# Order within an attention phase: transposes directly behind the scores, then corrections and outputs, then dense work

## The chip, the cores and the metric

The kernel runs on one core of one Trainium2 chip. Its time is the device time of one execution in microseconds. The kernel before took 1176.37 us in the median of 3 runs (1174.56 to 1176.48).

## What is computed

One decoder layer on a sequence of 1024 tokens of width 1024, all in float32. Two token mixers share one input projection and are merged by gates:

```python
h = rmsnorm(x, ln_pre);  z = h @ w_in        # columns of both mixers and of all gates
ya = conformer_conv(c_val, c_glu, ...)       # depthwise convolution, 31 taps, LayerNorm, swish, projection
ya = (ya * silu(c_gate)) @ w_br_conv
yb = sliding_window_sink_attention(q, k, v, sinks, positions)
yb = (yb * silu(a_gate)) @ w_br_attn
m = sigmoid(g_conv) * ya + sigmoid(g_attn) * yb
x = x + rmsnorm(m @ w_out, ln_post)
x = x + sigmoid(x @ w_ple_gate) * (p @ w_ple_proj)
```

The attention has 16 query heads of 64, two key and value heads, a window of 128 and one sink per head. The sequence is cut into 8 blocks of 128 queries; a block sees its own 128 keys and the 128 before, masked to the window, so that each query sees just 128 keys.

## The kernel before, in words

Activations lie transposed: features on the 128 partitions, tokens along the free axis. Every dense product is made in three passes: the weights and the activations are each split into a rounded high part and a low rest, and high by high, low by high and high by low are summed. A tile of 128 output features is 8 weight blocks by 3 passes by 2 halves of 512 tokens, that is 48 matmuls (L457). 114 tiles follow one another, with weights loaded one tile ahead into two slots; ScalarE makes the high part (L818) and VectorE the low part (L1158).

The attention is woven into the dense work of one gate, c_gate: 8 dense tiles are cut into 16 halves of 24 matmuls (L727), and each half makes a *phase* with one attention step, `attention(p)` for p = 0 to 15. Phase p belongs to query block n = p // 2 and to the half g = p % 2 of the heads. One block of attention work passes through several phases:

- Phase p, TensorE: `scores(p, 0)` and `scores(p, 1)` (L645) write the scores into PSUM. Where VectorE or ScalarE still read the old scores, they wait.
- VectorE: maxima of the scores (L1376, L1379), with the sinks (L1385 to L1389). ScalarE: the exponentials (L962, L967). VectorE: `normalise(p)` divides by the sums, in two halves (L1403); each half adds one to `probs_ready`.
- Phase p+1, TensorE: `turn(p)` transposes the normalised probabilities in 16 instructions (L663). It waits for both halves of `normalise(p)` and, by `half_evicted(p)`, until ScalarE has copied the gate half of phase p out of PSUM (L991).
- ScalarE: `copy_turned(p)` copies the transposes to SBUF (L948, L950), and VectorE masks a part of them (L1414) for the corrections.
- Phase p+2, TensorE: `outputs(p)` makes the outputs: from block n = 1 on first 8 correction matmuls (L697, with the differences `vstep` of neighbouring values, which VectorE makes once, in L1440 to L1444), then 8 output matmuls (L702). It waits by `half_evicted(p + 1)`, for the copies and the masks of step p, and for the outputs of step p-1 to have been copied away. ScalarE copies the outputs out in `copy_outputs(p)` (L975), which waits for `outputs(p)` and for `turn(p + 1)`, because both write the same banks.

So in phase p TensorE has five kinds of work: scores of p, corrections and outputs of p-2, transposes of p-1, and the dense half (for which `half_evicted(p - 2)` must hold). Their order in the queue is written out by hand in `attention`. In phases 1 and 2 the transposes stand within the dense half (in front of its weight block 6 or 5) instead, and phase 2 makes `outputs(0)` directly behind its scores.

The engines run on their own queues and wait by semaphores. ScalarE's order in phase p is: gate half p-1 (L988, L991), in every second phase the next weights' high part, `copy_outputs(p - 2)`, `copy_turned(p - 1)`, `exps(p)`. VectorE's is: maxima of p, gate half p-1 (L1428), extras of single phases (rotary parts in 0 to 2, `vstep` in 3, `sums_lo` in 14), masks of p-1 with the low part of weights between, `normalise(p)`.

Of the kernel before, what the change touches and what calls it, by code (L numbers as in the profile page):

```python
# [71 lines left out]
def build(nc, dram):  # L72
    with ExitStack() as ctx:
# [188 lines left out]
        def gate_bank(p):  # L262

            return psg_banks[:, 3 * (p % 2), :]
# [9 lines left out]
        def turn_place(p, side, jp):  # L274

            if p == LAST_P:
                return 2 + side, jp * QUARTER
            if side == 0:
                return whole_bank(p), jp * QUARTER
            return bank_pair(p).start + jp, 0  # L280
# [165 lines left out]
        def _(pe):  # L446
# [203 lines left out]
            def turn(p):  # L650

                g = p % 2
                pe.wait_ge(probs_ready, 2 * p + 2)
                if p < LAST_P:
                    half_evicted(p)
                if p in (1, LAST_P):
                    pe.wait_ge(o_ready, p)
                for jp in range(2):
                    for h in range(4):
                        for side in range(2):  # L660
                            queries = slice(side * HD, side * HD + HD)
                            bank, first = turn_place(p, side, jp)
                            mm = nc.tensor.transpose(psg_banks[:, bank, first + h * HD:first + h * HD + HD],  # L663
                                                     probs[g][queries, 4 * jp + h, :], ident[queries, queries])
                mm.then_inc(turned, 1)

            def half_evicted(p):

                n, h = divmod(p, 2)
                if h == 0:  # L670
                    pe.wait_ge(half_free, n + 1)
                else:
                    pe.wait_ge(ps_free[n % 2], (C0 + n) // 2 + 5)

            def out_of(p, side, par):

                return psg_banks[par * HD:(par + 1) * HD, bank_pair(p + 1).start + side, QUARTER:HALF]

            def heads_of(turned_rows, par):

                return turned_rows.rearrange("p (jp par j) q -> p par jp (j q)", jp=2, par=2)[:, par]

            def outputs(p):

                n, g = divmod(p, 2)
                gs = slice(g * HD, (g + 1) * HD)
                if p < LAST_P:
                    half_evicted(p + 1)
                if p > 0:
                    pe.wait_ge(o_ready, p)  # L690
                if n > 0:
                    pe.wait_ge(pt_masked, 2 * p - 2)
                    pe.wait_ge(vstep_ready, 3)
                    for side in range(2):
                        rows = slice(side * HD, side * HD + HD)
                        for par in range(2):
                            nc.tensor.matmul(out_of(p, side, par), vstep[rows, n - 1, gs], heads_of(pt_prev[rows], par),  # L697
                                             start=True, stop=False)
                pe.wait_ge(pt_copied, 2 * p + 2)
                for side in range(2):  # L700
                    for par in range(2):
                        mm = nc.tensor.matmul(out_of(p, side, par), vmix[:, n, gs], heads_of(pt_all[:, side], par),  # L702
                                              start=(n == 0), stop=True)
                mm.then_inc(pv_done, 1)

            def attention(p):

                n, h = divmod(p, 2)
                t = C0 + n
                half = slice(h * HALF, (h + 1) * HALF)  # L710
                scores(p, 0)
                scores(p, 1)
                if p > 1:
                    outputs(p - 2)
                if p > 2:
                    turn(p - 1)
                if h == 0:
                    pe.wait_ge(w_lo_ready, t + PLE_STEPS + 1)
                if n == 0:
                    pe.wait_ge(ps_free[h], C0 // 2 + 4)  # L720
                else:
                    half_evicted(p - 2)
                for k in range(KT):
                    if (p, k) in ((1, 6), (2, 5)):
                        turn(p - 1)
                    for m, (w, r) in enumerate(((w_hi, h_hi), (w_lo, h_hi), (w_hi, h_lo))):
                        mm = nc.tensor.matmul(gate_bank(p), w[:, t % 2, k * P:(k + 1) * P], r[:, k, half],  # L727
                                              start=(k == 0 and m == 0), stop=(k == KT - 1 and m == 2))
                mm.then_inc((half_done, tile_done)[h], 1)

            for p in range(2 * NB):
                attention(p)
# [941 lines left out]
```

## Time and profile before

| | us |
|---|---|
| Time, median of 3 runs | 1176.37 |
| Profiled execution, its time | 1176.3 |
| Its span, first to last instruction | 1174.5 |
| TensorE matmuls busy | 1164.0 |
| VectorE busy | 837.9 |
| ScalarE busy | 377.3 |
| L727 in the chain that ended last | 7% of the span |
| Granted clock of TensorE, mean | 0.998 |

The profile shows one execution. Busy time is the time in which an engine has an instruction in work; matmuls overlap, so a busy TensorE can still lose time between them, and the distance from start to start tells more than a duration. The phases p = 0 to 15 run from 488.9 us to 636 us of the span.

### The profile page before, as it was taken

How to read it: one execution, taken by the hardware profiler on the slowest of the kernel's cores; microseconds unless marked ns; L12 is line 12 of the kernel's file. 1: busy time of each engine (PE TensorE's matmuls, PEld its weight loads, DVE VectorE, ACT ScalarE, POOL GpSimd, SP SyncE). 2: the span in 40 equal slices, each digit the busy share in tenths (PEclk: the TensorE clock that was granted, in tenths of full speed). 3: DMA queues.
4: the chain of work that ended last, by engine and by line, in shares of the span. 5: the costliest groups of instructions: out<-in, count | busy, mean ns of one | idle time of the engine just before them, and what ended most of it. 6: DMA issues, size and time to landing. Idle time of an engine off the chain costs nothing.

```text
span 1174.5 us, 16083 instructions
## 1 busy us (share of the span) xinstructions
PE 1164.0 (99%) x6304; PEld 947.3 (81%) x6304; DVE 837.9 (71%) x934; ACT 377.3 (32%) x670; POOL 17.4 (1%) x17
## 2 busy tenths in 40 slices
PE   9999999999999999989999999999999999999998
PEld 7788888888888888867777888888888888888886
DVE  6999999999999983788777674783233344357665
ACT  6431221221121122266665442341122112444331
POOL 1020000000000000000000000000000000000000
PEclk9999999999999999999999999999999999999999
DMA  9622122222222323212122111333232232434655
GB/s 353 267 90 71 55 88 72 62 81 71 71 72 77 93 54 87 53 55 73 38 73 74 36 54 36 107 107 90 89 107 89 90 107 88 127 115 139 210 164 179
DMA packets 35530, 116.40 MB, mean 99 GB/s; under 512 B 4480, under 2 KB 4992, under 8 KB 35488
## 3 DMA queue, kind: packets, MB, share of 16 engines
q1 hardware_dynamic: 25120, 82.29, 22.1%
q10 hardware_dynamic: 10368, 33.56, 8.6%
q8 instruction: 26, 0.43, 0.2%
q14 instruction: 16, 0.13, 0.0%
HBM read 92.10 MB, written 20.97 MB: 96 GB/s over the span
## 4 chain that ended last, share of the span: by engine, by line
PE 94%; DMA 2%; ACT 1%; DVE 1%; SPq 1%; issue 0%; POOL 0%; ACTq 0%; DVEq 0%
PE psg L457 81%; PE psg L727 7%; PE psg L702 1%; PE psb L645 1%; DMA k_raw<-positions 1%; DMA x_rows<-x_rows 1%; PE psg L663 1%; PE psg L697 1%; PE psg L506 1%; ACT probs L962 0%; DVE w_lo L1158 0%; SPq L366 0%; PE psb L530 0%; PE psb L540 0%; SPq L363 0%
## 5 line engine op out<-in xcount | busy, mean ns | idle before, releaser
L457 PE MATMUL psg<-h_hi,w_hi 128*128 128x512 f32 x768 | 237.1, 390 | 0.5 <-DVE w_lo L1158 0.5
L457 PE MATMUL psg<-h_hi,w_lo 128*128 128x512 f32 x768 | 236.6, 389 | 0.0
L457 PE MATMUL psg<-h_lo,w_hi 128*128 128x512 f32 x768 | 236.4, 389 | 0.0
L818 ACT ACTIVATE w_hi<-w_raw 128x1024 fp32r<-128x1024 f32 x112 | 118.5, 1058 | 223.7 <-PE psg L457 211.4
L1158 DVE TENSOR_TENSOR w_lo<-w_raw,w_hi 128x1024 fp32r<-128x1024 f32 x114 | 139.1, 1221 | 70.0 <-ACT w_hi L818 69.9
L457 PEld LDWEIGHTS psg<-h_hi,w_hi 128*128 128x128 f32 x768 | 143.7, 188 | 31.1 <-issue 1.6
L457 PEld LDWEIGHTS psg<-h_hi,w_lo 128*128 128x128 f32 x768 | 144.2, 188 | 30.1
L457 PEld LDWEIGHTS psg<-h_lo,w_hi 128*128 128x128 f32 x768 | 144.1, 188 | 30.1
L1298 DVE SCALAR_TENSOR_TENSOR conv<-u,cols,conv 128x1024 f32<-128x1024 f32 x120 | 154.0, 1284 | 0.0
L1298 DVE SCALAR_TENSOR_TENSOR work<-u,cols,work 128x1024 f32<-128x1024 f32 x112 | 145.5, 1299 | 0.0
L727 PE MATMUL psg<-h_hi,w_hi 128*128 128x512 f32 x128 | 52.1, 407 | 0.0
L727 PE MATMUL psg<-h_hi,w_lo 128*128 128x512 f32 x128 | 50.2, 392 | 0.0
L1546 DVE TENSOR_TENSOR work<-psg,ring 128x1024 f32<-128x1024 f32 x8 | 9.8, 1225 | 56.5 <-PE psg L457 56.5
L727 PE MATMUL psg<-h_lo,w_hi 128*128 128x512 f32 x128 | 50.0, 391 | 0.0
L457 PE MATMUL psg<-x_hi,w_hi 128*128 128x512 f32 x128 | 49.9, 390 | 0.0
L457 PE MATMUL psg<-x_lo,w_hi 128*128 128x512 f32 x128 | 49.8, 389 | 0.0
L457 PE MATMUL psg<-x_hi,w_lo 128*128 128x512 f32 x128 | 49.8, 389 | 0.0
L457 PE MATMUL psg<-m_hi,w_hi 128*128 128x512 f32 x112 | 43.8, 391 | 0.2 <-DVE w_lo L1158 0.2
L457 PE MATMUL psg<-m_lo,w_hi 128*128 128x512 f32 x112 | 43.6, 389 | 0.0
L457 PE MATMUL psg<-m_hi,w_lo 128*128 128x512 f32 x112 | 43.6, 389 | 0.0
L1554 DVE SCALAR_TENSOR_TENSOR work<-ring,psg 128x1024 f32<-128x1024 f32 x8 | 9.8, 1221 | 46.8 <-PE psg L457 46.8
L962 ACT ACTIVATE probs<-psb,nmax 128x128 f32<-128x128 f32 x112 | 39.6, 402 | 1.4 <-DVE esink L1389 1.4
(223 smaller groups left out, 1732.1 us busy)
## 6 DMA issues: line engine op xcount, KB each, us to landing
w_raw<-weights SPq DMA_DIRECT2D x114, 512.0 KB, 3.6
gates<-ring ACTq DMA_DIRECT2D x24, 512.0 KB, 2.7
ring<-gates ACTq DMA_DIRECT2D x24, 512.0 KB, 3.7
x_rows<-x_rows SPq DMA_DIRECT2D x8, 512.0 KB, 9.7
conv<-xT SPq DMA_DIRECT2D x8, 512.0 KB, 14.4
ple<-ple_out SPq DMA_DIRECT2D x8, 512.0 KB, 13.6
x_ring<-xT ACTq DMA_DIRECT2D x16, 256.0 KB, 3.5
ple_all<-ple ACTq DMA_DIRECT2D x8, 512.0 KB, 4.0
```

Source lines behind the costliest of these rows:

```text
L457: mm = nc.tensor.matmul(psg[:, slot, h * HALF:(h + 1) * HALF], w[:, wslot, (wk + k) * P:(wk + k + 1) * P], r[:, k, h * HALF:(h + 1) * HALF ...
L506: mm = nc.tensor.matmul(psg[:, slot, cols_h], w[:, slot, k * P:(k + 1) * P], r[:, k, cols_h], start=(k == 0 and n == 0), stop=(k == KT - 1 ...
L645: mm = nc.tensor.matmul(psb[out_rows, 2 * jp + par, j2 * 2 * P + first:j2 * 2 * P + first + width], qo[rows, 4 * g + 2 * jp + j2, queries] ...
L663: mm = nc.tensor.transpose(psg_banks[:, bank, first + h * HD:first + h * HD + HD], probs[g][queries, 4 * jp + h, :], ident[queries, queries])
L697: nc.tensor.matmul(out_of(p, side, par), vstep[rows, n - 1, gs], heads_of(pt_prev[rows], par), start=True, stop=False)
L702: mm = nc.tensor.matmul(out_of(p, side, par), vmix[:, n, gs], heads_of(pt_all[:, side], par), start=(n == 0), stop=True)
L727: mm = nc.tensor.matmul(gate_bank(p), w[:, t % 2, k * P:(k + 1) * P], r[:, k, half], start=(k == 0 and m == 0), stop=(k == KT - 1 and m == 2))
L818: nc.scalar.activation(w_hi[:, j % 2, :], w_raw[:, j % 2, :], ACT.Copy).then_inc(w_hi_ready, 1)
L962: ex = nc.scalar.activation(probs[g][:, h, :], src, ACT.Exp, bias=nmax[:, head], scale=SCALE, accum_out=denom[:, head])
L1158: nc.vector.tensor_tensor(w_lo[:, slot, :], w_raw[:, slot, :], w_hi[:, slot, :].bitcast(F32), ALU.subtract).then_inc(w_lo_ready, 1)
L1298: own.step(stt(dst, src[:, j:j + S], tap(j), dst, ALU.mult, ALU.add))
L1546: nc.vector.tensor_tensor(work[:], psg[:, j, :], ring[:, j, :], ALU.mult).then_inc(ps_free[j], 1)
```

## The change

In the phases from 3 on, `turn(p - 1)` and `outputs(p - 2)` change places in TensorE's queue. Phase 2, which has only `outputs(0)` there, keeps it.

```diff
                 scores(p, 0)
                 scores(p, 1)
-                if p > 1:
+                if p == 2:
+                    outputs(0)
+                elif p > 2:
+                    turn(p - 1)
                     outputs(p - 2)
-                if p > 2:
-                    turn(p - 1)
                 if h == 0:
                     pe.wait_ge(w_lo_ready, t + PLE_STEPS + 1)
```

## Rows read from the trace of the kernel before

**Rows 1.** The page's chain that ended last, shares by engine.
```profile
PE 94%; DMA 2%; ACT 1%; DVE 1%; SPq 1%; issue 0%; POOL 0%; ACTq 0%; DVEq 0%
```

**Rows 2.** Timeline, phase 8: start us, us, engine, line, work, count [idle before]; PEld weight loads.
```profile
562.94 1.32 PE L645 MATMUL psb<-kdup,qo 64*32 64x160 f32 x64
564.19 0.21 PEld L697 LDWEIGHTS psg<-pt_prev,vstep 64*64 64x64 f32 x8 [0.25 <-ACT gate_val L991]
564.78 0.63 PEld L702 LDWEIGHTS psg<-pt_all,vmix 128*64 128x64 f32 x8 [0.38 <-issue]
565.79 0.57 PEld L663 LDWEIGHTS psg<-ident,probs 64*128 64x128 f32 x16 [0.38 <-issue]
566.43 0.19 PEld L727 LDWEIGHTS psg<-h_hi,w_hi 128*128 128x128 f32 x1
```

**Rows 3.** Timeline, phase 3: scores' second half, outputs, weight loads of the transposes.
```profile
517.98 0.78 PE L645 MATMUL psb<-kdup,qo 64*32 64x160 f32 x32 [0.53 <-ACT probs L962]
519.05 1.08 PE L702 MATMUL psg<-pt_all,vmix 128*64 128x256 f32 x8 [0.29 <-ACT gate_val L991]
...
520.06 0.57 PEld L663 LDWEIGHTS psg<-ident,probs 64*128 64x128 f32 x16 [0.38 <-DVE probs L1403]
```

**Rows 4.** Timeline of TensorE: phase 4's corrections, its dense work, phase 5's corrections.
```profile
527.60 0.66 PE L697 MATMUL psg<-pt_prev,vstep 64*64 64x256 f32 x8
...
529.85 0.50 PE L727 MATMUL psg<-h_hi,w_hi 128*128 128x512 f32 x1
...
530.65 0.39 PE L727 MATMUL psg<-h_hi,w_hi 128*128 128x512 f32 x1
...
536.75 0.66 PE L697 MATMUL psg<-pt_prev,vstep 64*64 64x256 f32 x8
```

**Rows 5.** Timeline of VectorE: normalise(2), masks, normalise(3).
```profile
518.49 1.29 DVE L1403 TENSOR_TENSOR probs<-probs,rden 128x512 f32<-128x512 f32 x2
...
525.90 1.41 DVE L1414 TENSOR_TENSOR pt_prev<-pt_all,mixed 64x512 f32<-64x512 f32 x2
...
527.78 1.29 DVE L1403 TENSOR_TENSOR probs<-probs,rden 128x512 f32<-128x512 f32 x2
```

**Rows 6.** Timeline of TensorE in the tile behind the phases: outputs, then dense work.
```profile
638.07 1.08 PE L702 MATMUL psg<-pt_all,vmix 128*64 128x256 f32 x8
639.08 0.74 PE L457 MATMUL psg<-h_hi,w_hi 128*128 128x512 f32 x2
```

**Rows 7.** Timeline of ScalarE: gate copy and transposed copy, exponentials of 3, next transposed copy.
```profile
518.33 0.66 ACT L991 ACTIVATE gate_val<-psg 128x512 f32<-128x512 f32 x1
...
521.85 0.60 ACT L950 ACTIVATE pt_all<-psg 128x512 f32<-128x512 f32 x1
...
525.84 0.24 ACT L967 ACTIVATE esink<-esink 128x8 f32<-128x8 f32 x1
...
531.00 0.60 ACT L950 ACTIVATE pt_all<-psg 128x512 f32<-128x512 f32 x1
```

**Rows 8.** Timeline, phase 7: transposed copy, last exponential, normalise.
```profile
558.44 0.60 ACT L950 ACTIVATE pt_all<-psg 128x512 f32<-128x512 f32 x1
...
561.65 0.27 ACT L967 ACTIVATE esink<-esink 128x8 f32<-128x8 f32 x1
...
562.40 1.29 DVE L1403 TENSOR_TENSOR probs<-probs,rden 128x512 f32<-128x512 f32 x2
```

**Rows 9.** Timeline, phase 15: normalise(14), weight loads of the corrections.
```profile
626.75 1.29 DVE L1403 TENSOR_TENSOR probs<-probs,rden 128x512 f32<-128x512 f32 x2
...
628.21 0.21 PEld L697 LDWEIGHTS psg<-pt_prev,vstep 64*64 64x64 f32 x8 [0.25 <-ACT gate_val L991]
```

**Rows 10.** Timeline of TensorE in phase 2: outputs, then the fourth dense matmul.
```profile
507.11 1.98 PE L702 MATMUL psg<-pt_all,vmix 128*64 128x256 f32 x8 [2.48 <-ACT gate_val L991]
...
510.44 0.40 PE L727 MATMUL psg<-h_hi,w_hi 128*128 128x512 f32 x1
```

**Rows 11.** Table of stretches, phase 2: length, engines' busy us (x), granted clock, DMA.
```profile
508.00:509.00 1.00, 1.00 (x6) 0.24 (x2) 0.96 (x3) 0.00 (x1) 0.00 (x0) 0.50 0.00 0
```

## Prediction

> **What bounds the kernel now.** I read the chain of waits first: 94% of the span is TensorE [rows 1]. So the end moves by what TensorE gains or loses, and the question is only where its queue would stand still.
>
> Next the timeline of one ordinary phase, p = 8, by start times [rows 2]: scores 562.94, corrections 564.19, outputs 564.78, transposes 565.79, dense 566.43. From start to start that is 1.25, 0.59, 1.01 and 0.64 us. The phase repeats every 9.15 us (corrections at 527.60 and 536.75) [rows 4].
>
> Then the first phases that the change touches, p = 3 [rows 3] and p = 4 [rows 4], beside VectorE's timeline [rows 5]. In phase 3 the weight load of the transposes names VectorE's normalisation (L1403) as what ended its idle time of 0.38 us; the same 0.38 in phase 8 is put down to nothing, only "issue" [rows 2]. The normalisations ended at 518.49 + 1.29 = 519.78 and 527.78 + 1.29 = 529.07, well behind the starts of the first step after the scores, 519.05 and 527.60. In the old order corrections and outputs fill TensorE while VectorE finishes; that is the cover which the change takes away.
>
> **The change part by part.** Nothing is added or removed: in phases 3 to 15, 13 of them, the 16 transposes of block p-1 move ahead of the output matmuls of block p-2 and, from p = 4, of the corrections before those (8 instructions each). They issue no DMA and pass no other engine's queue. Phase 2 keeps its order. With the transposes moves their wait for both halves of normalise(p-1); the wait for the gate half's copy stands ahead of whichever comes first. Behind the waiting transposes now stand outputs, dense matmuls and the next scores; ScalarE's L975 waits for outputs and transposes both, in either order.
>
> Step 1, the matmuls themselves. A change of kind costs TensorE a drain, and the drain goes with the block that ends: outputs take 1.01 us up to transposes [rows 2] and 1.01 up to dense work (639.08 - 638.07) in the tile after the phases [rows 6]. Transposes take 0.64 up to dense, scores 1.25 to the next kind [rows 2]. The one boundary that no row shows is transposes to corrections. From below, the next weights could be loaded while the transposes still run: their loads last 0.57 of the 0.64, and the last of 16 matmuls can hardly end its share (0.64 / 16 = 0.04) later than about 0.5 after the start, so 0.15 a phase is the most there is to gain. From above, the loads could stand idle 0.25 us as between scores and corrections, instead of the 0.07 ahead of dense work (566.36 to 566.43): 0.18 lost [rows 2]. Twelve phases have that boundary: -1.8 to +2.2 us. I take 0, as the blocks that the rows do show keep their length whatever follows.
>
> The Trainium skill, "TensorE: Matmul & The Clock Gate", Part 2, says that TensorE's queue pulls weight loads ahead of matmuls in flight where row groups don't conflict. Transposes and corrections both use half the rows, so by that rule the boundary would take the lower end, -1.8. The idle of 0.25 between scores and corrections, half-row tiles too, ends with the gate's copy, so no row here confirms or refutes it; it is a rival below.
>
> Step 2, phase 3. A release reaches TensorE 0.06 us after it (the gate's copy ends 518.33 + 0.66 = 518.99, the outputs start at 519.05) [rows 3, 7]. By the gate the transposes could start at 519.05; the normalisation lets them go at 519.78 + 0.06 = 519.84. Transposes and outputs then take 0.64 + 1.01 as before: dense work starts 0.79 us late.
>
> Step 3, phase 4. VectorE does not feel that: it works on from 518.49 to 529.07 (maxima, gate half, the vstep differences, masks, normalise) [rows 5], and its inputs are in time even later. The transposed copies end at 521.85 + 0.60 + 0.79 = 523.24, wanted at 525.90. The exponentials begin some 0.2 later, behind that copy, so end near 525.84 + 0.24 + 0.2 = 526.3, wanted at 527.31, where the masks end [rows 5, 7]. So normalise(3) still ends at 529.07, and the transposes go at 529.13. By TensorE's own order they would go at 527.60 + 0.79 = 528.39. Another 0.74 us [rows 4, 5].
>
> Step 4, phase 5. Scores, gate copy and L975 now run 0.79 + 0.74 = 1.53 late. ScalarE's copy ends at 531.00 + 0.60 + 1.53 = 533.13 [rows 7]. From the end of that copy to the end of the exponentials a steady phase takes 561.92 - 559.04 = 2.88, so 536.01; from there to the end of normalise 563.69 - 561.92 = 1.77 [rows 8]: 537.78, transposes allowed at 537.84. Their place is at 536.75 + 1.53 = 538.28 [rows 4]. Nothing more is lost.
>
> Step 5, phases 6 to 15. Here the loop closes through outputs: transposes, corrections, outputs, L975, copies, exponentials, normalise, next transposes. L975 starts when the later of the two blocks is through; 0.64 + 0.59 + 1.01 is the same sum in either order, so it stays where it is. The steady normalise ends at 563.69, its release lands at 563.75, the slot is at 564.19 [rows 2, 8]: 0.44 us spare, which also covers that an output matmul runs longer through the array than a transpose. Phase 15 is the tightest: 626.75 + 1.29 + 0.06 = 628.10 against 628.21 [rows 9], 0.11 spare, and both move together. Were that cover gone, its lateness would count once.
>
> Sum: 0.79 + 0.74 = 1.53 us. Behind the phases TensorE is the bound to the end, so nothing gives it back. The profiled execution took 1176.3 us (a span of 1174.5 and 1.8 around it), with the change 1177.8; the median of the runs shown, 1176.37, stands 0.07 above it: 1177.9 us.
>
> **The rivals.** *The clock falls.* In phase 2 TensorE stood still for 2.48 us, and right behind that its granted clock was 0.50 (1.2 instead of 2.4 GHz) [rows 10, 11]. The change puts an idle stretch of about 1.1 us into phase 3 (scores done near 518.76, transposes at 519.84) behind the 0.53 that is there [rows 3]. The price, from rows at both levels: outputs and three dense matmuls took 510.44 - 507.11 = 3.33 instead of 1.01 + 0.80 (529.85 to 530.65) [rows 4, 10]: 1.5 us, giving 1179.4. For it: the clock was given back only shortly before. Against it: behind the present stalls of 0.53 and 0.29 the outputs of phase 3 take 1.01 us to the transposes, the length at full clock, and the new one is less than half of 2.48.
>
> The Trainium skill, same page, Part 1, "What's actually happening", says that activity releases the throttle and idleness brings it back; the fall in phase 2 agrees.
>
> *The steady phases pay as well.* The boundary of transposes to corrections costs 0.1 us in twelve phases, inside the bound of step 1: +1.2, so 1179.1. For it: no row shows it, and more waits than one stand at it. Against: block lengths that don't depend on what follows.
>
> *It becomes faster, or comes out even.* If that boundary is cheaper instead, by overlapping loads, each of the twelve phases gives back up to 0.15. It decides from 1.53 / 12 = 0.13 each; at the full 0.15 the time is 1176.37 + 1.53 - 1.8 = 1176.1. For it: both kinds are small tiles. Against: every boundary that the rows show drains the block in front.
>
> *The order does nothing.* If normalise(2) and (3) ended before the slots, the blocks would simply change places: 1176.4. Against it: the ends 519.78 and 529.07.
>
> **How the numbers follow.** Forecast 0.66, clock 0.11, steady cost 0.11, faster or even 0.07, no effect 0.05. What a measurement of this kernel can tell from no change is 0.2%, 2.35 us, so slower begins at 1178.7 and faster at 1174.0. The forecast lies inside; the clock and the steady cost lie beyond, 0.22 together, and the spread of single executions (the runs before span 1174.56 to 1176.48) adds about what it takes: slower 0.23. Faster 0.04, from spread alone, as even the favourable rival stays inside; same 0.73. The range reaches from 1176.1, the favourable rival, to 1179.5, just past the clock; the upper end of the unknown boundary, 1180.1, is left out.
>
> **What would show it.** Phase 3: transposes about 0.8 us behind the gate copy, with L1403 as releaser. Phase 4: an idle of some 0.7 us beyond the drain, again L1403. From phase 5: the period of 9.15 us back, transposes 1.25 behind the scores' start, corrections 0.64 behind them, and L975 released by the outputs (L702) instead of the transposes. L1403 as releaser in phases past 5 would make me wrong towards slow; a phase below 9.15 us, or a phase 3 without that wait, towards fast; a second stretch at 0.50 would be the clock.

## The result and the profile after

The changed kernel took 1179.03 us in the median of 19 executions (1177.61 to 1180.53), the kernel before 1176.31 (1174.56 to 1176.66, 19 executions beside them): 2.72 us more by the medians, and a ratio of 1.0028 with a 95% interval of 1.0021 to 1.0035. It is slower, by more than the 0.2% that a measurement tells from no change, and nearly twice the forecast's 1.53 us.

The times of either kernel lie in groups, and the clock of TensorE explains them. Before: 8 executions from 1174.56 to 1175.48 and 11 from 1176.12 to 1176.66. After: 2 below 1178, 13 from 1178.51 to 1179.62, 4 from 1179.94 up. The profiled execution of before, with one fall of the clock in phase 2 [rows 11], took 1176.3 and is of the upper group; that of the changed kernel, with two falls, took 1179.94 and is of the top group. Four kernels below have a profile without a fall in the phases; three of these executions are of their kernel's lower group, and the fourth kernel has a single group. The mean clock of each execution is on record too: after, it is 1.000 in the 2 lowest, 0.998 or 0.999 in the 13, 0.996 or 0.997 in the 4 on top. In 66 more executions of the kernel before, which stand beside the experiments, it is 0.999 or 1.000 in the 26 up to 1175.52, 0.998 in the 35 from 1175.72 to 1177.08, and 0.997 in 5 from 1177.78 to 1178.45. So like is compared with like, by the means of the groups: no fall 1174.9 and 1177.8 (only 2 executions), one fall 1176.4 and 1179.0, that is 2.6 to 2.9 us.

Lines of the new kernel behind the change are one higher (L727 is now L728, L991 now L992). First its phase 7 in the timeline, weight loads as PEld, which answers to [rows 2]:

```profile
556.50 1.32 PE L645 MATMUL psb<-kdup,qo 64*32 64x160 f32 x64
...
557.10 0.59 ACT L992 ACTIVATE gate_val<-psg 128x512 f32<-128x512 f32 x1
...
557.81 0.60 PEld L663 LDWEIGHTS psg<-ident,probs 64*128 64x128 f32 x16 [0.31 <-issue]
...
558.48 0.21 PEld L697 LDWEIGHTS psg<-pt_prev,vstep 64*64 64x64 f32 x8
...
559.08 0.63 PEld L702 LDWEIGHTS psg<-pt_all,vmix 128*64 128x64 f32 x8 [0.39 <-issue]
...
560.09 0.19 PEld L728 LDWEIGHTS psg<-h_hi,w_hi 128*128 128x128 f32 x1 [0.39 <-issue]
560.21 0.60 ACT L976 ACTIVATE qo<-psg 128x512 f32<-128x512 f32 x1 [2.51 <-PE psg L702]
```

Transposes to corrections take 0.67 by the loads, outputs to dense 1.01. But from the scores' start to the transposes' first load it is 1.31, and 1.34 to their first matmul, where the old order had 1.25 to the corrections. The gate's copy ends at 557.69, 1.19 after the scores' start, as before (554.98 - 553.79 in phase 7). The scores of phase 4 start at 528.74 and those of phase 7 at 556.50, so the period is 9.25 us instead of 9.15, in every phase to the last.

Then the timeline of TensorE in phases 3 and 4, which answers to [rows 3, 4]:

```profile
516.67 0.78 PE L645 MATMUL psb<-kdup,qo 64*32 64x160 f32 x32 [0.40 <-ACT probs L963]
517.98 0.78 PE L645 MATMUL psb<-kdup,qo 64*32 64x160 f32 x32 [0.52 <-ACT probs L963]
519.84 0.72 PE L663 MATMUL psg<-ident,probs 64*128 64x64 f32 x16 [1.09 <-DVE probs L1404]
520.49 1.93 PE L702 MATMUL psg<-pt_all,vmix 128*64 128x256 f32 x8
522.35 0.80 PE L728 MATMUL psg<-h_hi,w_hi 128*128 128x512 f32 x1
...
528.74 1.32 PE L645 MATMUL psb<-kdup,qo 64*32 64x160 f32 x64
530.08 0.71 PE L663 MATMUL psg<-ident,probs 64*128 64x64 f32 x16
530.72 0.66 PE L697 MATMUL psg<-pt_prev,vstep 64*64 64x256 f32 x8
```

The transposes of phase 3 start at 519.84, as worked out, released by the normalisation. Behind them the outputs take 1.86 us to the dense work instead of 1.01. The table of stretches (length, busy us of the engines, then the granted clock, DMA) shows why:

```profile
519.00:520.00 1.00, 0.16 (x4) 0.16 (x6) 1.00 (x3) 0.00 (x0) 0.00 (x0) 1.00 1.01 414
521.00:522.00 1.00, 1.00 (x8) 0.40 (x4) 0.96 (x3) 0.00 (x0) 0.00 (x0) 0.50 0.00 0
522.00:523.00 1.00, 1.00 (x4) 0.56 (x3) 0.90 (x5) 0.54 (x2) 0.00 (x0) 0.50 0.00 0
```

In this execution the clock fell a second time, to 0.50 (1.2 instead of 2.4 GHz), behind the idle stretch of 1.09 us. That delayed the scores of phase 4 so far that the normalisation was ready for its transposes: no stall there.

### The profile page after: what moved, and what is told of

Its sections match the earlier page's. It is cut to its first block, busy times and chain, and to the rows that moved or that the text cites. A ratio compares the mean times of both kernels' runs of the same rounds, so it can differ in the third digit from the quotient of the medians.

```text
span 1178.2 us, 16083 instructions
## 1 busy us (share of the span) xinstructions
PE 1166.6 (99%) x6304; PEld 948.4 (80%) x6304; DVE 838.7 (71%) x934; ACT 377.0 (32%) x670; POOL 17.3 (1%) x17
## 4 chain that ended last, share of the span: by engine, by line
PE 94%; DMA 2%; ACT 1%; DVE 1%; SPq 1%; issue 0%; POOL 0%; ACTq 0%; DVEq 0%
PE psg L457 81%; PE psg L728 8%; PE psg L702 2%; PE psb L645 1%; DMA k_raw<-positions 1%; DMA x_rows<-x_rows 1%; PE psg L663 1%; PE psg L697 1%; PE psg L506 1%; ACT probs L963 0%; DVE w_lo L1159 0%; SPq L366 0%; PE psb L530 0%; PE psb L540 0%; DVE probs L1404 0%
## 5 line engine op out<-in xcount | busy, mean ns | idle before, releaser
L728 PE MATMUL psg<-h_hi,w_hi 128*128 128x512 f32 x128 | 52.6, 411 | 0.0
L728 PE MATMUL psg<-h_hi,w_lo 128*128 128x512 f32 x128 | 50.5, 394 | 0.0
L728 PE MATMUL psg<-h_lo,w_hi 128*128 128x512 f32 x128 | 50.2, 392 | 0.0
```

## Experiments

Eight kernels, in two sets of four; each has 11 executions, and beside each set the kernel before has 33, with medians of 1176.20 and 1176.17. Their intervals are about 0.2% wide (2 us), so where tenths of a microsecond matter, the verdict rests on the distances in the profile, which repeat to 0.02 us. Line numbers differ by a few between kernels. Kernels are counted in the order below; the edits of the fourth and the eighth are shown against the kernel before, the others against the changed kernel.

**New order in phases 5 to 15 only.**

```diff
-                elif p > 2:
+                elif p > 4:
                     turn(p - 1)
                     outputs(p - 2)
+                elif p > 2:
+                    outputs(p - 2)
+                    turn(p - 1)
```

> New order in phases 5 to 15 only, phases 3 and 4 in the old one. Theory S (the time is lost only where the normalisation is late, phases 3 and 4): the same as before, 0.0 us, period 9.15. Theory W (each phase with the new order pays about 0.1 us between scores and transposes, 1.34 from start to start instead of 1.25): 11 phases by 0.10, +1.1 us, period 9.25. Theory C (the clock falls once more behind the idle stretch of phase 3, and that is the excess over the forecast): no such stretch here, 0.0 us, and one fall at most, in phase 2.

Measured: 1177.88 us, ratio 1.0014 [1.0005, 1.0023]. Timeline of TensorE, phases 5 to 7:

```profile
535.61 1.32 PE L645 MATMUL psb<-kdup,qo 64*32 64x160 f32 x64
537.32 0.71 PE L663 MATMUL psg<-ident,probs 64*128 64x64 f32 x16 [0.39 <-DVE probs L1407]
...
545.23 1.32 PE L645 MATMUL psb<-kdup,qo 64*32 64x160 f32 x64
546.57 0.71 PE L663 MATMUL psg<-ident,probs 64*128 64x64 f32 x16
...
554.48 1.32 PE L645 MATMUL psb<-kdup,qo 64*32 64x160 f32 x64
```

1.34 and 9.25 in each phase from 6 on: theory W. What none had said: phase 5 now pays 0.46 (1.71). TensorE comes to it without the delay of phases 3 and 4, and normalise(4) ends at 537.26, behind the place of the transposes at 535.61 + 1.25 = 536.86. It is as late in the kernel before, where corrections and outputs, from 536.75 on, cover it (timeline of VectorE, kernel before):

```profile
535.89 1.29 DVE L1403 TENSOR_TENSOR probs<-probs,rden 128x512 f32<-128x512 f32 x2
```

It ends at 537.18 there. 0.46 and ten phases by 0.106 make 1.5 of the 1.68 us.

**New order in phases 3 and 4 only** (the condition is `p in (3, 4)`).

> New order in phases 3 and 4 only. Theory S: all of the loss is here, near the measured +2.7 us of the medians. Theory W: stalls of 1.53 and the dearer boundary once, in phase 4, so +1.6 us, and a period of 9.15 from phase 5 on. Theory C: +1.5 where the clock stays, about +2.3 in an execution in which it falls a second time in phase 3 (the stall of phase 4 then vanishes behind the slow stretch).

Measured: 1177.90 us, ratio 1.0017 [1.0007, 1.0026]. The profiled execution has the fall of phase 2 and none in phase 3. Timeline of TensorE:

```profile
516.87 0.78 PE L645 MATMUL psb<-kdup,qo 64*32 64x160 f32 x32 [0.40 <-ACT probs L966]
...
520.04 0.71 PE L663 MATMUL psg<-ident,probs 64*128 64x64 f32 x16 [1.09 <-DVE probs L1407]
...
527.37 1.32 PE L645 MATMUL psb<-kdup,qo 64*32 64x160 f32 x64
529.33 0.71 PE L663 MATMUL psg<-ident,probs 64*128 64x64 f32 x16 [0.65 <-DVE probs L1407]
...
537.26 1.32 PE L645 MATMUL psb<-kdup,qo 64*32 64x160 f32 x64
538.51 0.66 PE L697 MATMUL psg<-pt_prev,vstep 64*64 64x256 f32 x8
```

Scores to transposes 1.96 in phase 4, 0.71 more than 1.25 (forecast 0.74). From the scores of phase 3 to those of phase 5 it is 20.39, in the kernel before 535.50 - 516.67 = 18.83: 1.56 us lost in both (forecast 1.53), 1.25 and 9.15 from there on.

**The gate's wait written first** in the changed kernel's transposes.

```diff
-                pe.wait_ge(probs_ready, 2 * p + 2)
                 if p < LAST_P:
                     half_evicted(p)
+                pe.wait_ge(probs_ready, 2 * p + 2)
```

> The changed kernel, with the two waits of the transposes written in the other order: first the copy of the gate half, then the normalisation. Theory W, in the form that the wait written first is carried by the weight load and the other one by an instruction of its own ahead of it: scores to transposes back at 1.25, period 9.15, +1.5 to +1.6 us against the kernel before instead of +2.7. Theory L (the transposes start later behind the scores because of their kind of tile, whatever they wait for): no difference from the changed kernel, +2.7 us, 1.34.

Measured: 1178.26 us, ratio 1.0016 [1.0007, 1.0025]. Timeline of TensorE:

```profile
547.20 1.32 PE L645 MATMUL psb<-kdup,qo 64*32 64x160 f32 x64
548.45 0.71 PE L663 MATMUL psg<-ident,probs 64*128 64x64 f32 x16
549.09 0.66 PE L697 MATMUL psg<-pt_prev,vstep 64*64 64x256 f32 x8
...
556.36 1.32 PE L645 MATMUL psb<-kdup,qo 64*32 64x160 f32 x64
```

Two lines exchanged, and 1.34 is 1.25 again, the period 9.16. Theory L falls. The trace's records of semaphore instructions, which the profile doesn't count as work, show the mechanism (us from the span's start):

```
changed kernel, phase 7                  gate's wait first, phase 7
557.694  gate's copy ends                557.208  separate wait, normalisation
557.732  separate wait, gate (51 ns)     557.552  gate's copy ends
557.809  weight load, normalisation      557.604  weight load, gate
```

Of several waits ahead of a matmul, the one written first is carried by its weight load, and the others become instructions of their own ahead of it (one such instruction can hold two of them, as in the next kernel). If the late one is among those, its release has to pass that instruction before the load can go: 115 ns behind the copy's end instead of 52. Separate waits that are through before the late release cost nothing: in phase 7 of the kernel before two of them stand at 554.643 and 554.754, the gate's copy ends at 554.985, and the load that carries the gate's wait starts 54 ns later.

This kernel's profile also has two falls of the clock, the second in phase 3; it is of the 7 executions from 1178.19 to 1179.02, while 4 took 1176.49 to 1177.07. The three of these with a mean clock of 1.000 lie near 1176.7, 1.8 above the lower group of the kernel before: the 1.5 of the forecast, 0.09 more in phase 3 (3.26 from scores to transposes instead of 3.17), where the normalisation is late and now stands in the separate wait, and about 0.01 a phase.

**The old order, the gate's wait not first.**

```diff
-                if p < LAST_P:
-                    half_evicted(p + 1)
-                if p > 0:
-                    pe.wait_ge(o_ready, p)
                 if n > 0:
                     pe.wait_ge(pt_masked, 2 * p - 2)
                     pe.wait_ge(vstep_ready, 3)
+                if p < LAST_P:
+                    half_evicted(p + 1)
+                if p > 0:
+                    pe.wait_ge(o_ready, p)
+                if n > 0:
                     for side in range(2):
```

> The kernel before in its old order, but the outputs' waits written so that the copy of the gate half isn't first (the masks are). Theory W in the same form: scores to corrections from 1.25 to about 1.31, 12 phases, +0.8 to +1.2 us. Theory L: no difference from the kernel before, 0.0 us.

Measured: 1178.73 us, ratio 1.0020 [1.0011, 1.0029]. Timeline of TensorE:

```profile
545.01 1.32 PE L645 MATMUL psb<-kdup,qo 64*32 64x160 f32 x64
546.46 0.66 PE L698 MATMUL psg<-pt_prev,vstep 64*64 64x256 f32 x8
...
554.36 1.32 PE L645 MATMUL psb<-kdup,qo 64*32 64x160 f32 x64
```

1.45 instead of 1.25, a period of 9.35: W's direction, but 0.2 a phase and not 0.06 to 0.1. The records of phase 7 show two separate waits behind the gate's copy here (555.554 copy ends, waits at 555.591 and 555.702, load at 555.779). The first holds the gate; the second holds the two waits for `vstep` and for the earlier outputs, which were released long before and are now queued behind the late one. One in series costs some 0.06 us to the load and 0.09 to the matmul, two 0.17 and 0.2. Twelve phases by 0.2 make 2.4 of the 2.53 us.

**New order in phase 4 only** (the condition is `p == 4`).

> New order in phase 4 only. Theory D (the stall of phase 4 is set by VectorE's own time line: normalise(3) ends some 10.5 us after normalise(2) starts, whatever TensorE did in phase 3): without the delay of phase 3 the transposes wait the full 529.13 - 527.60 = 1.53 us, so scores to transposes 2.78 and +1.5 to +1.6 us, as much as phases 3 and 4 together. Theory A (each phase has a stall of its own, which add up): 0.7 us more in phase 4, +0.7 us.

Measured: 1176.46 us, ratio 1.0013 [1.0004, 1.0022]. The median misleads here: 7 of 11 executions are of the group without a fall, 1176.15 to 1176.58, 1.5 above the lower group of the kernel before, near 1174.8. Timeline of TensorE:

```profile
524.99 1.32 PE L645 MATMUL psb<-kdup,qo 64*32 64x160 f32 x64
527.76 0.71 PE L663 MATMUL psg<-ident,probs 64*128 64x64 f32 x16 [1.46 <-DVE probs L1407]
```

2.77, so 1.52 lost in one phase: theory D. A late VectorE makes one deadline that TensorE runs into, in phase 3, in phase 4 or in parts (and, less late, in phase 5, as the first kernel shows); the stalls don't add up.

**New order from phase 5, the gate's wait first** (the edits of the first and third kernel).

> New order in phases 5 to 15 with the gate's wait written first, old order in phases 3 and 4. Theory W: the order of the blocks itself is free, the period is 9.15, and only phase 5 pays, by the 0.46 us less the 0.09 of the separate wait that it lost already with the late-only kernel: +0.4 us. Theory L (blocks of transposes cost more ahead of corrections than behind outputs): about +1.1 us more, as in the late-only kernel.

Measured: 1176.86 us, ratio 1.0002 [0.9993, 1.0011]: not told from no change by that. Like with like it is 0.7 us above the kernel before (5 executions near 1175.5 against 1174.8 without a fall, 6 near 1177.2 against 1176.5), which is the loss of phase 5 and about 0.01 a phase. Timeline of TensorE, phases 5 to 7:

```profile
533.96 1.32 PE L645 MATMUL psb<-kdup,qo 64*32 64x160 f32 x64
535.78 0.72 PE L663 MATMUL psg<-ident,probs 64*128 64x64 f32 x16 [0.50 <-DVE probs L1407]
...
543.72 1.32 PE L645 MATMUL psb<-kdup,qo 64*32 64x160 f32 x64
544.96 0.71 PE L663 MATMUL psg<-ident,probs 64*128 64x64 f32 x16
...
552.88 1.32 PE L645 MATMUL psb<-kdup,qo 64*32 64x160 f32 x64
```

The order of the blocks itself is free but for about 0.01: 1.24 or 1.25, and 9.16. Phase 5 loses 0.57 (1.82) instead of the expected 0.4 to 0.5, because there the separate wait is the late one.

**The lateness covered with dense work**, phases 3 to 5 (on the third kernel; `pt_copied` and `o_ready` are waited for ahead of the dense half, since it shares a bank with what they guard).

```diff
+                elif p in (3, 4, 5):
+                    pe.wait_ge(pt_copied, 2 * p - 2)
+                    pe.wait_ge(o_ready, p - 2)
                 elif p > 2:
...
+                    if (p, k) in ((3, 2), (4, 3), (5, 2)):
+                        turn(p - 1)
+                        outputs(p - 2)
```

> The changed order with the gate's wait first, but in phases 3, 4 and 5 transposes and outputs stand within the dense half (ahead of its weight block 2, 3, 2), so that dense matmuls cover VectorE's lateness. Theory C (the second fall of the clock comes from the idle stretch of 1.1 us in phase 3): no fall in phase 3, no idle time on L663, about +0.2 us against the kernel before (three dense halves cut in two at some 0.2 us each, less the 0.3 us that TensorE waits for the gate's copy in phase 3). If the clock falls in phase 3 all the same, the idle stretch isn't its cause.

Measured: 1177.98 us, ratio 1.0015 [1.0006, 1.0024]; the cost was missed. Timeline of TensorE, phase 6, then a stretch of phases 3 and 4:

```profile
543.92 1.32 PE L645 MATMUL psb<-kdup,qo 64*32 64x160 f32 x64
546.10 0.72 PE L663 MATMUL psg<-ident,probs 64*128 64x64 f32 x16 [0.86 <-DVE probs L1410]
```

```profile
518.00:524.00 6.00, 6.00 (x44) 4.38 (x43) 5.80 (x11) 3.44 (x15) 0.00 (x0) 1.00 0.12 46
```

The transposes of phases 3 to 5 no longer stall and the clock stays, but outputs inside the dense half come later, and with them ScalarE's copies and exponentials: the scores of phase 5 wait 0.37 for exponentials (1.62 from scores to dense work), normalise(5) is late, and phase 6 pays 0.93. A cut dense half costs 0.27, not 0.2 (phase 4 takes 9.41 instead of 9.15). Without a fall the kernel stands 1.8 above the kernel before (1176.6 against 1174.8). That the clock didn't fall in phase 3 of this one profile doesn't settle the cause of a second fall: it didn't in that of the second kernel either, which has the idle stretch.

**Phases 2 to 4 rewoven, the old order from 5** (with the gate's wait first, as in the third kernel).

```diff
-                if p > 1:
-                    outputs(p - 2)
-                if p > 2:
-                    turn(p - 1)
+                if 2 <= p <= 4:
+                    pe.wait_ge(pt_copied, 2 * p - 2)
+                    if p > 2:
+                        pe.wait_ge(o_ready, p - 2)
+                elif p > 4:
+                    outputs(p - 2)
+                    turn(p - 1)
...
+                    if (p, k) == (2, 3):
+                        outputs(0)
                     if (p, k) in ((1, 6), (2, 5)):
                         turn(p - 1)
+                    if (p, k) in ((3, 3), (4, 3)):
+                        turn(p - 1)
+                        outputs(p - 2)
```

> A version meant to beat both: phases 2, 3 and 4 begin their dense half behind the scores at once, with outputs(0) ahead of weight block 3 in phase 2, transposes then outputs ahead of block 3 in phases 3 and 4; from phase 5 the old order. TensorE's 2.48 us of idleness in phase 2 should go, and with it the fall of the clock there; what is late next is VectorE's normalise(2), which can come 2.6 us earlier (its idle time ahead of L1396 in phase 3). Expected -2.5 to -3.5 us against an execution of the kernel before in which the clock fell, -1 to -2 against one in which it did not. If scores(3) then wait for the exponentials as long as phase 2 did for the gate's copy, it comes out even.

Measured: 1174.08 us (1173.64 to 1174.56), ratio 0.9986 [0.9977, 0.9996], the only kernel faster than the one before. Timeline of TensorE in phases 2 and 3, then a stretch of phase 2:

```profile
502.90 1.32 PE L645 MATMUL psb<-kdup,qo 64*32 64x160 f32 x64
506.70 1.08 PE L702 MATMUL psg<-pt_all,vmix 128*64 128x256 f32 x8 [0.19 <-ACT gate_val L999]
...
512.77 0.78 PE L645 MATMUL psb<-kdup,qo 64*32 64x160 f32 x32 [0.49 <-ACT probs L970]
514.08 0.78 PE L645 MATMUL psb<-kdup,qo 64*32 64x160 f32 x32 [0.53 <-ACT probs L970]
```

```profile
506.00:512.00 6.00, 5.81 (x42) 3.80 (x40) 5.73 (x15) 4.13 (x11) 0.00 (x0) 1.00 0.19 72
```

The idle time of phase 2 goes from 2.48 to 0.19 us, and all 11 executions lie within 0.9 us: no second group. That gains 2.1 to 2.3 us on an execution of before with a fall and 0.7 on one without, less than was expected: phases 4 and 5 give some back (their scores take 1.61 and 1.98 to the next block).

## Why the prediction was wrong, point by point

*What bounds it* was right: what TensorE lost in the phases, 2.73 us by the sum below, came back in the time.

*Step 1* failed. I took "scores 1.25 to the next kind" for the transposes too, although the only row for it had corrections behind the scores. It is 1.34, and the period 9.25: 0.106 us in each of some 12 phases, 1.2 to 1.3 us. The unknown boundary that I bounded, transposes to corrections, costs what I took (0.64 from matmul to matmul, nothing extra). I had written that the wait for the gate's copy "stands ahead of whichever comes first" and did not ask in which form. The third and fourth kernel show that the form is the price.

*Steps 2 and 3* were right: 519.84, 0.79 and 0.71 for 0.79 and 0.74, together 1.56 for 1.53, by the kernel with phases 3 and 4 only. *Step 4* held: phase 5 of that kernel is at 1.25, and normalise(4) ends there at 537.92; its times run 0.20 later than those of the kernel before, so that is 537.72 for the 537.78 of the forecast. But the step reckoned with ScalarE's copy and a steady phase alone. By VectorE's own time line, which it left out, normalise(4) ends at 537.18 in the kernel before, behind the place at 536.75; that nothing was lost hung on the delay of 1.53, and the kernels with TensorE on time in phase 5 lose 0.46 and 0.57 there. *Step 5* held for the loop through ScalarE: L976 is released by L702, and behind phase 5 L1404 is named once only, in phase 15, for 0.31 us. There the normalisation ended at 631.49 and the gate's copy at 631.72, and the distance is 1.34 as in the other phases.

*The sum:* 1.56 and eleven phases by 0.106 (the twelfth, phase 4, waits for the normalisation anyway) make 2.73 us, against the 2.72 of the medians.

*The rivals.* "The steady phases pay as well" had the size (+1.2, 1179.1) and the wrong place. "The clock falls" comes true in some executions on top: in the profiled one transposes to next scores take 8.90 us in phase 3, in the kernel with phases 3 and 4 only, with the same idle stretch and no fall, 7.33. The 1.57 agrees with the price of 1.5; some 0.65 of it is not extra, since the stall of phase 4 goes. That the idle stretch brings the fall is not shown: two of the three profiles with a stretch of 1.09 or 1.18 us have the second fall, and none of the seven others has one in phase 3; but 5 of the 66 executions of the kernel before, without the stretch, have the mean clock of two falls too, and no profile shows where theirs fell.

"Faster or even" fell: the transposes take their 0.64 us to the corrections as to dense work. The Trainium skill, "TensorE: Matmul & The Clock Gate", Part 2, lets weight loads be pulled ahead where row groups don't conflict; at this boundary the trace shows no gain from it. "The order does nothing" fell with the two stalls.

The chances were wrong with the step: 0.23 for slower, because the form of a wait had no term of its own. That 1179.03 lies inside the range of 1176.1 to 1179.5 is luck: the range reached so far up for the clock, not for the wait.

*Left open:* why the dense half takes 5.66 instead of 5.65 in the new order, about 0.01 a phase; what brings the second fall of the clock; and whether one separate wait in the old order would cost exactly the 0.1 it costs in the new.

## What to carry to other kernels

Before a block is moved in a queue, look at what fills the queue while its input is made: here corrections and outputs were 1.6 us of cover for a normalisation that came late in three phases, 3 to 5. Where several waits stand ahead of a matmul, write the one that is released last first, and check the distance from block to block in every phase: 0.1 us by 11 phases, 1.2 us, was nearly as much as the 1.56 of the two visible stalls. The idle stretch worth removing was the long one, in phase 2, that the change did not touch.

## What the runs showed of the hardware that I had not expected

- A wait of its own ahead of a weight load costs time when its release is the late one: 1.34 us instead of 1.25 from scores to the next block. A second one queued behind it costs as much again, 1.45, though its own release was early. Separate waits that are through before the late release cost nothing (1.25 in the kernel before, with two of them).
- The order of kinds of matmul costs no more than about 0.01 us a phase by itself: scores, transposes, corrections, outputs take 1.25, 0.64, 0.59, 1.01 us from start to start in either order, with the gate's wait first.
- One program has two or three levels of time, 1.5 us apart, by how often the clock falls to 0.50; in the profiles each fall in the phases comes at the end of a stall of TensorE or right behind it (2.48 us in phase 2, 1.09 or 1.18 in phase 3), and the same stalls also pass without one. The kernel whose stall in phase 2 is gone has one level.
